# Layer 0 of a hybrid decoder trunk in a new order: phase tables made while x loads, norms first, projections in turn with recurrence steps, and another order of the mixer's tail

## The reference

```python
h = rms_norm(x, norm1)
z = h @ w_in                       # u_a (512), v_b (1024), u_c (512), gates (3 x 1024)
gates = sigmoid(z[..., o3:] + b_gate)
y_a = s5_mixer(u_a, ...) @ ssm_w_proj
y_b = conv_module(v_b, ...)        # GLU, causal depthwise conv of 31 taps, LayerNorm, silu, @ w_proj
y_c = pool_mixer(u_c, ...)         # causal means over 2, 4, 8, 16, minus u_c, grouped matmul, @ w_proj
x = x + (gates[0]*y_a + gates[1]*y_b + gates[2]*y_c) @ w_out
h = rms_norm(x, norm2)
x = x + (silu(h @ w_gate) * (h @ w_up)) @ w_down
```

## Time and profile before

| | us |
|---|---|
| median of 3 runs | 2200.13 (2188.8 to 2464.33) |
| profiled execution | 2193.92 |
| its span (core 5, the slowest; cores 2175.1 to 2192.4) | 2192.4 |
| TensorE busy | 2013.1 |
| VectorE busy | 1013.1 |
| ScalarE busy | 663.8 |

### The profile page before, as it was taken

The page is one execution under the profiler, slowest core; times in us unless marked ns, Lnnn a source line. Parts: engine busy times, 40 slices in busy tenths (PEclk is TensorE's granted clock), DMA queues, the critical chain, the costliest instruction groups (busy, mean ns, idle before and its releaser), DMA issues.

```text
span 2192.4 us, 31111 instructions; the slowest of 8 cores (2175.1 to 2192.4 us)
## 1 busy us (share of the span) xinstructions
PE 2013.1 (92%) x11536; PEld 926.8 (42%) x11536; DVE 1013.1 (46%) x1484; ACT 663.8 (30%) x1104; POOL 85.6 (4%) x160
## 2 busy tenths in 40 slices
PE   2767879999999999999997977999999999999997
PEld 1333344444444444444443434444444444444443
DVE  5647746444454444442252773644445423223226
ACT  3651255222234202314242225622223310110123
POOL 1000000000000000000000000000000000000000
PEclk9978999999999999999998989999999999999998
DMA  9342515222143214224256361522214321322203
GB/s 229 58 103 71 104 28 106 39 39 39 20 135 68 49 29 77 49 54 100 39 190 141 97 121 30 107 39 39 37 22 135 58 39 20 58 39 39 39 10 154
DMA packets 56659, 156.31 MB, mean 71 GB/s; under 512 B 5952, under 2 KB 26816, under 8 KB 53440
## 3 DMA queue, kind: packets, MB, share of 16 engines
q0 software_dynamic: 21456, 77.05, 21.0%
q1 hardware_dynamic: 30448, 73.07, 10.2%
q10 hardware_dynamic: 4608, 4.20, 0.8%
HBM read 191.48 MB, written 27.26 MB: 100 GB/s over the span
## 4 chain that ended last, share of the span: by engine, by line
PE 86%; DVE 5%; ACT 3%; issue 3%; DMA 1%; ACTq 1%; SPq 0%; DVEq 0%
PE ps L257 86%; DVE gt L227 1%; DVE h L235 1%; DMA tab_mid<-ph 1%; ACTq L273 1%; DVE tmp L227 1%; ACT po L246 1%; DMA ud<-stg 0%; ACT sq_s L246 0%; SPq L273 0%; ACT g L246 0%; ACT ps L246 0%; ACT ph L246 0%; DVE lt L227 0%; DVE cv L227 0%
## 5 line engine op out<-in xcount | busy, mean ns | idle before, releaser
L257 PE MATMUL ps<-h,slot 128*128 128x512 bf16 x5376 | 1216.0, 383 | 28.3 <-DVE h L235 18.6
L257 PEld LDWEIGHTS ps<-h,slot 128*128 128x128 bf16 x5376 | 528.0, 99 | 673.0 <-issue 56.5
L227 DVE TENSOR_TENSOR actb<-ps,sgf 128x512 bf16<-128x512 f32 x176 | 121.6, 692 | 418.6 <-PE ps L257 381.5
L257 PE MATMUL ps<-actb,slot 128*128 128x512 bf16 x1408 | 305.9, 379 | 0.0
L246 ACT ACTIVATE sgf<-ps 128x512 f32<-128x512 f32 x176 | 104.8, 595 | 579.6 <-PE ps L257 567.2
L246 ACT ACTIVATE gt<-ps,hb 128x512 f32<-128x512 f32 x192 | 131.4, 686 | 344.8 <-PE ps L257 343.2
L235 DVE SCALAR_TENSOR_TENSOR acc<-gt,ps 128x512 f32<-128x512 f32 x180 | 123.4, 688 | 238.9 <-PE ps L257 235.9
L257 PEld LDWEIGHTS ps<-actb,slot 128*128 128x128 bf16 x1408 | 137.7, 98 | 165.9
L227 DVE TENSOR_TENSOR x<-ps,x 128x512 f32<-128x512 f32 x192 | 130.3, 690 | 133.3 <-PE ps L257 133.2
L264 POOL DMA_DIRECT2D slot<-wts x146 | 77.6, 535 | 1950.3 <-PE ps L257 1911.9
L257 PE MATMUL ps<-mg,slot 128*128 128x512 bf16 x512 | 119.8, 398 | 5.6 <-DVE mg L235 5.6
(11 more groups left out here) (126 smaller groups left out, 1202.7 us busy)
## 6 DMA issues: line engine op xcount, KB each, us to landing
slot<-wts POOLq DMA_DIRECT2D x146, 512.0 KB, 6.8
x<-xT SPq DMA_DIRECT2D x16, 512.0 KB, 18.2
x<-xT SPq DMA_DIRECT2D x4, 2048.0 KB, 19.2
x_mid<-x SPq DMA_DIRECT2D x4, 2048.0 KB, 8.1
x<-x_mid SPq DMA_DIRECT2D x4, 2048.0 KB, 19.2
outT<-x SPq DMA_DIRECT2D x4, 2048.0 KB, 6.3
tab_mid<-ph SPq DMA_DIRECT2D x24, 256.0 KB, 3.4
tab<-tab_mid SPq DMA_DIRECT2D x6, 1024.0 KB, 4.9
```

Of the source, the lines that this page charges most:

```text
L227: return (eng or dve).put(lambda e: e.tensor_tensor(out=out, in0=a, in1=b, op=op), after)
L257: ins = e.matmul(out, lhsT=a, rhs=b, start=start and i == 0, stop=stop and i == n - 1, **kw)
```

## The change

1. **Phase tables.** `rot` becomes part of the beginning of `gens(0)`. The first four phase pairs get a buffer each (in the place of `uc`, not used yet) and are made while x loads, between the small passes for `pk`; SP copies them to `tab`. The last four are made in `tab` itself, by `step(S["rots"])` inside `scan(1)` and `scan(2)`. Layer 0 writes nothing to `tab_mid`.
2. **Norms first.** Squares and `finish` of blocks 0 and 1 come before u; the rest of `gens(0)` moves behind. The `ud` scatter of layer 0 is issued by SP and not by ScalarE, and `k_mid` by ScalarE and not by SP.
3. **u, p, c in turn.** The recurrence of layer 0 starts in the second half of p. In layer 1 all of p comes before c, with 2 steps per part of p from the fifth on and 3 per half-block of c. `out_mats` come before all of `inside`.
4. **Banks.** `bank` takes the bank used longest ago, and `quad` the quad whose last use is oldest (before: a counter).
5. **Tail.** All pool sums stand before conv(0); `cv` has four places of its own (and GT, ACC change theirs); conv(2) goes before glu(0), conv(3) between glu(1) and glu(2), and ln_silu(0) and (1) behind the fold. In the weight order `glu` goes from behind cd 4 to behind cd 6.

The core of the diff (its repeated renamings are left out):

```diff
@@ slot_order
-    if l == 0:
-        order = u + p + c
-    else:
-        order = u + [c[0], p[0], c[1], c[2], p[1], c[3]]
-    order += cd[:5] + [("glu", 0)] + cd[5:] + [("wpc", 0), ("wpc", 1)]
+    order = u + p + c + cd[:7] + [("glu", 0)] + cd[7:] + [("wpc", 0), ("wpc", 1)]
@@ places
-    CV = at("cv", [2, 4, 512], F32, o_rb)
+    CV = [at("cv%d" % i, [4, 512], F32, o) for i, o in enumerate((o_rb, o_rb + 8192, o_x, o_x + 8192))]
-    ACC = [at("acc%d" % i, [3, 512], F32, o_rb + 8192 * i) for i in range(2)]
-    GT = [at("gt%d" % i, [512], F32, o_x + 2048 * i) for i in range(8)]
+    ACC = [at("acc%d" % i, [3, 512], F32, o_x + 8192 * i) for i in range(2)]
+    GT = [at("gt%d" % i, [512], F32, o_rb + 2048 * i) for i in range(8)]
@@ banks
+    def bank():
+        i = min(turn["from"], key=lambda i: turn["at"][i])
+        turn["gen"] += 1
+        turn["at"][i] = turn["gen"]
+        return i
+    def quad():
+        k = min((k for k in (0, 4) if k in turn["from"]), key=lambda k: max(turn["at"][k:k + 4]))
+        turn["gen"] += 1
+        turn["at"][k:k + 4] = [turn["gen"]] * 4
+        return [k, k + 1, k + 2, k + 3]
@@ gens: rot moved to the front, and
+                if l == 0:
+                    t_ld.append([ta, tb])
+                    yield
+                    continue
+        ra = out["ra"] = iter(()) if l else rot(0, 4)
@@ scan
+            drain(S["rots"])
+            want_tabs()
+            rots = iter(())
+            if l == 0 and pt in (1, 2):
+                for i in range(2):
+                    out["ph_free"][2 * pt + 2 + i] = [S["tab_free"][1 - pt % 2]]
+                rots = out["rot"](2 * pt + 2, 2 * pt + 4)
@@ layer 0
-            for b in range(NB):
-                for _ in p_blk(b):
-                    step(g0, 2)
-            turn["from"] = [4, 5, 6, 7]
...
-            for b in range(NB):
-                for i, _ in enumerate(c_blk(b)):
-                    step(g0, 3)
-                    step(sc, 4)
-                    if i == 1 and b:
-                        pool_sums(b - 1)
...
+            for k, _ in enumerate(all_of(p_blk)):
+                step(g0, 1)
+                if k == 7:
+                    turn["from"] = [4, 5, 6, 7]
+                if k >= 7:
+                    step(sc, 2)
+            while "re" not in out:
+                step(g0)
+                step(sc, 2)
...
+            for k, _ in enumerate(all_of(c_blk)):
+                step(g0, 2)
+                want_tabs()
+                step(sc, 4)
+                if k == 5:
+                    pool_edge()
@@ layer 1
-            for _ in range(8):
-                step(cs)
-                step(sc, 3)
-                for _ in range(2):
-                    step(pb)
-                    step(sc, 1)
-            for _ in cs:
-                step(sc, 3)
+            for k, _ in enumerate(all_of(p_blk)):
+                if k > 3:
+                    step(sc, 2)
+                    want_tabs()
+            for _ in all_of(c_blk):
+                step(sc, 3)
+                want_tabs()
@@ tail
+        for m in range(4):
+            pool_sums(m)
         conv(0)
         ln_sum(0)
         conv(1)
         ln_sum(1)
         st2(0)
         ln_stat(0)
         st2(1)
-        st2(2)
         ln_stat(1)
-        st2(3)
         ln_rs(0)
         ln_rs(1)
         ln_apply(0)
         ln_apply(1)
+        st2(2)
+        st2(3)
+        conv(2)
         glu(0)
+        ln_sum(2)
         glu(1)
-        ln_silu(0)
-        ln_silu(1)
-        conv(2)
-        glu(2)
-        ln_sum(2)
-        glu(3)
-        conv(3)
-        ln_stat(2)
-        ln_sum(3)
+        conv(3)
+        glu(2)
+        ln_sum(3)
+        glu(3)
         fold([slot(l, "wpc", h) for h in range(2)])
+        ln_stat(2)
+        ln_stat(3)
+        ln_silu(0)
+        ln_silu(1)
```

More of the change, by code:

```diff
@@ L210, in build_program @@
     W1ST = at("w1st", [4, 2, 2, 128], BF16, o_rb + 4096)
-    KSTS = [[at("kst%d" % i, [4, 2, 128], BF16, o_x + 40960 + 2048 * i) for i in range(4)],
+    KSTS = [[at("kst%d" % i, [4, 2, 128], BF16, o_x + 40960 + 2048 * (i % 3)) for i in range(4)],
             [at("kst", [4, 2, 128], BF16, o_rb + 8192)] * 4]
@@ L615, in gens @@
         out["re"] = [free[0], free[1], free[2], out["kpe"], wc[3][-1]]
-        if l == 0:
-            yield from rot(4, 8)
-        else:
-            ph_free = {n: out["re"] for n in range(3)}
-            out["tab"] = t_ld
+        if l:
+            ph_free.update({n: out["re"] for n in range(3)})
             yield from rot(0, 8)
-        out["end"] = t_ld[5] + t_ld[6] + t_ld[7] + out["w1"] + out["k"]
+        out["end"] = (t_ld[5] + t_ld[6] + t_ld[7] if l else []) + out["w1"] + out["k"]
     def step(g, n=1):
@@ L841, in load_tab, with want_tabs @@
         def load_tab(pt):
+            if l == 0 and pt > 1:
+                S["tab"][pt] = out["tab"][2 * pt] + out["tab"][2 * pt + 1]
+                return
+            if l == 0:
+                pairs = [(TAB[pt][:, k, 2 * i:2 * i + 2], PHS[0][2 * pt + i][:, 1 - k]) for i in range(2) for k in range(2)]
+                S["tab"][pt] = [dmas(sp, pairs, d_tabl[pt], out["tab"][2 * pt] + out["tab"][2 * pt + 1] + S["x1_free"])]
+                S["rd_free"] = S["rd_free"] + S["tab"][pt]
+                return
             S["tab"][pt] = [dma(sp, TAB[pt % 2][:, :], s_tab[l, pt], d_tabl[pt % 2],
                                 [S["tab_free"][pt % 2]] + out["tab"][2 * pt] + out["tab"][2 * pt + 1] + S["x1_free"])]
+        def want_tabs():
+            for pt in range(4):
+                if S["tab"][pt] is None and len(out["tab"]) >= 2 * pt + 2 and pt < S["scanned"] + 2:
+                    load_tab(pt)
         def st2(pt):
@@ L1037, in x_places, with all_of @@
                 S["pt"] = dma(pool, PT[:, :], d_pt[:, :], d_pt_sem, S["x3_free"])
-        def begin_ssm():
-            load_tab(0)
-            load_tab(1)
+        def all_of(blk):
+            for b in range(NB):
+                yield from blk(b)
         def ssm():
@@ L1062, in finish @@
                 x_places()
-            step(g0, 10)
+            step(g0, 6)
+            ra = out["ra"]
+            step(ra, 1)
             squares(0)
+            step(ra, 2)
             finish(0)
-            step(g0, 2)
-            squares(1)
-            S["ws_u"] = [slot(l, "u", c) for c in range(2)]
-            ub = u_blk(0)
+            squares(1)
+            step(g0, 1)
+            finish(1)
+            drain(ra)
+            step(g0, 3)
+            S["ws_u"] = [slot(l, "u", c) for c in range(2)]
@@ L1070, in layer @@
+            load_tab(0)
+            load_tab(1)
+            drain(u_blk(0))
+            step(g0, 2)
+            squares(2)
+            ub = u_blk(1)
+            step(ub, 1)
+            finish(2)
+            drain(ub)
+            squares(3)
+            step(g0, 4)
+            ub = u_blk(2)
+            step(ub, 1)
+            finish(3)
+            drain(ub)
+            step(g0, 4)
+            ub = u_blk(3)
             step(ub, 2)
-            finish(1)
             step(g0, 2)
             drain(ub)
-            squares(2)
@@ new lines, in layer @@
+            S["pads"] = [mset(pool, UC[:, :, :, 0:2], 0.0, S["rd_free"])]
+            S["ws_p"] = [slot(l, "p", c) for c in range(2)]
+            S["ws_c"] = [slot(l, "c", m) for m in range(4)]
+            sc = ssm()
+            S["w1"] = [out["w1"]] * 4
+            S["hp_free"] = lambda pt: S["stg_free"][(0, 1, 4, 5)[pt]]
+            for k, _ in enumerate(all_of(p_blk)):
+                step(g0, 1)
+                if k == 7:
+                    turn["from"] = [4, 5, 6, 7]
+                if k >= 7:
+                    step(sc, 2)
@@ L1186, in layer @@
         S["acce_free"] = [None, None]
+        S["gt_free"] = [S["yb"][i // 4][-1] for i in range(8)]
         ws = (slot(l, "mA", 0), slot(l, "mB", 0))
-        ln_stat(3)
+        merge(0, 0, ws, True)
         ln_rs(2)
         ln_rs(3)
-        merge(0, 0, ws, True)
         ln_apply(2)
@@ L1211, in layer @@
         t_last = last
-        x_load(0, [t_last] + S["gt_free"])
+        x_load(0, [t_last] + S["acc_free"])
         x_load(1, [t_last])
```

195 lines of the change are left out of this document (79 added, 116 removed).

## The result

The changed kernel took 2110.97 us (median of 4 runs, 2107.39 to 2366.68). The kernel before, run beside it, has a ratio to it of 0.9616 (after to before), 95% interval 0.9565 to 0.9667: faster. Disturbed runs are left out of every ratio here, which is why a ratio isn't the quotient of two medians. The profiled execution took 2113.91 us, 1.5 more than its span of 2112.4, 80.0 less than the one before.

What follows compares the result with a forecast made beforehand. TensorE was busy 2013.1 of 2192.4 us, so gains come from its 179 us idle and lower-clock stretches; 47 + 12.5 + 21 + 8.5 = 89 us off 2193.9 gives 2105 us, 8-in-10 range 2080 to 2142.

Steps and rivals of the forecast that it cites:

- The rest: Both merges, w_out and FFN: order kept, x_load(0) about 2 us later but covered by w_out; gain nothing.
- the VectorE budget: Layer 0: 112.0 us of VectorE work after 85.9, so 197.9, and 199 with the first st1.
- the first term: Layer 0 up to the first conv matmul: 212.6 against 259.95, 47 us gained, bounds 30 and 55.
- the second and third terms: Layer 0, conv(0) to merge: 12.5 us gained, bounds 6 and 16; layer 1 up to st2(0): 21, bounds 12 and 25.
- the fourth: Layer 1, st2(0) to merge: 13.5 us idle become 5 to 6; 8.5 gained, bounds 3 and 12.
- The front's walk: Layer 0's start: last norm result 5.0 us earlier, p begins at 86.6 instead of about 93.5, 7 us gained.
- The signs: Right if conv near 212, merge near 290, VectorE above nine tenths busy; wrong if stg waits exceed 1.5 us per half-block.
- the forecast's own case: The whole kernel gains as the terms say, 2105 us within 2080 to 2135; chance 0.76.
- c at 1.2 GHz: Rival, c of layer 0: VectorE's ring halves TensorE's clock, 35 us lost, 2140 us; chance 0.10.
- The early recurrence: Rival, layer 0: scans start only when the inside matrices end, 126 not 102; 24 us lost, 2129; chance 0.06.
- the lost lookahead: Rival, c in both layers: each half-block clears ScalarE and VectorE before the next; net 49 us slower, 2243; chance 0.03.
- The alternation of Sin and Tanh: Layer 0's c on ScalarE: charged nothing; by the skill's page eight switches would cost 21 us, up to 11 on the path.

Runs made afterwards that it cites:

- e4: The changed kernel with layer 1's output and inside matrices in the order of before; 2101.85 us, ratio 0.9594.
- e3: The changed kernel with layer 0's last two kst tiles in stg 3's place, so tg waits only for two k_mid transfers; 2107.55 us, ratio 0.9619.
- e2: The changed kernel with no layer 0 recurrence step ahead of the first c half-block; 2128.94 us, ratio 0.9716.
- best3_again: Rerun on another chip: changed kernel with the edits of e3 and e4 and three recurrence steps per layer 0 c half-block, not four; 2092.9 us, ratio 0.9564.
- e1: The changed kernel with the order of before from st2(0) on in both layers; 2122.07 us, ratio 0.9689.
- e9: The changed kernel with the old PSUM bank rule, a counter for single banks and quads in turn; 2131.93 us, ratio 0.9727.

## Why the prediction was right or wrong

The time was forecast at 2105 us with 2080 to 2142; it came to 2111. The sum was 89 us, the span shows 80. Most mechanisms held; two steps failed. The first is "The rest ... keeps its order ... Nothing": the FFN beside which layer 1's matrices are made did not keep its order, and 9.0 us were given back there (8.7 by e4). The second is the VectorE budget in the first term, 6.5 us too much: VectorE's total was taken for the bound of conv(0), and the wait of the first Tanh for `k_mid` (3.5 us by e3) was left out. That the sum missed by only 9 us is in part luck: on the slowest cores the second and third terms came out 3.1 and 3.8 us larger than forecast, the fourth 2.1 smaller, and 2.0 us behind layer 1's merge were in no term, beside 9.3 given back on these cores. (Merge is counted here, as in the prediction, from its first matmul; the table's marker is its third product.)

**Layer 0 to conv(0)**, 47 forecast, 40.5 on the slowest core (41.9 by the median). The front's walk held: the four `h` start at 29.67, 39.04, 60.17 and 72.43 (29.8, 39.3, 59.8, 72.3). The first recurrence step comes at 105.11, not near 102: VectorE waits 2.35 us for `wc`, queued behind evacuations on ScalarE. Two waits of 0.59 and 2.34 us for inside matmuls follow, then 3.58 for the Tanh behind `k_mid`, which the walk doesn't mention; e3 shows it cost 3.5. The c half-blocks at 4.7 us were right (139.64 to 208.65 is 4.6 each for 15), the allowance of 4 us for Tanh behind phase passes was used by those waits instead. The sums took 14.0 us (205.41 to 219.44) against 12.6 in the walk, with 72 matmuls at the lower clock. The false step is that VectorE must have finished all its steps ahead of conv(0): e2 and best3_again show the last steps under the sums and the conv, and so does the prediction's own figure for the kernel before, where the last recurrence ended at 274.9 us and conv(0) started at 259.95. The evacuation that ScalarE held behind the `tab_mid` stall was one of p and not of c (`stg` from ScalarE; c's first `tg` comes at 161.47); the stall and its end are as the prediction says.

**Conv(0) to merge of layer 0**, 12.5 forecast, 15.6 on the slowest core. The waits left were as named (1.68 for gelu's evacuation, about 3 in fold), the slot of `mB` 0 stayed hidden. Where it came from was half seen: 6.7 from the order (e1), 5.6 from the choice of banks (e9), the rest open.

**Layer 1.** Up to st2(0) 24.8 us less from st1(0) on (137.0 to 112.2), 21 forecast; to merge 6.4 less (68.9 to 62.5), 8.5 forecast. The mechanisms held: the five half-blocks of p took 5.2 us of work out of the stretch behind st1(0) (14.58 us of waiting became 4.32 and 6.10), and the sums' cover for hc is worth 10.4. Mis-sized was p's place, 12.2 us with the wait for `tmp` that it saves.

**The rest at nothing.** The 9.0 us given back beside the FFN come from an edit in `gens` that I had followed in layer 0 only.

**The signs.** conv(0) was at 219.4 and not near 212, merge at 293.8 (near 290 said), VectorE busy 87.33 of the 97 us from 102 to 199, just the nine tenths. TensorE waited 16.2 us for `stg` in c and ahead of the second sum, 1.0 per half-block; none of the signs of being wrong appeared. The range of the forecast's own case, 2080 to 2135, isn't the plain sum of the terms' bounds, which is 2086 to 2143.

**Rivals.** c at 1.2 GHz: no, the clock was 0.96 in 160 to 200. The early recurrence did happen, and its price is 6.3 us at conv(0), not 24. Of the lost lookahead there is no trace: the changed kernel waits 16.2 us for `stg`, the one with the old bank rule 19.1, each with its wait at the pool sums counted in. The alternation of Sin and Tanh costs nothing: between the load at 137.43 and the next at 238.37 ScalarE shows none, while `tab` and `tg` passes alternate. The rule of the Trainium skill (ScalarE: Activation LUTs, "Table sets: the hidden batching unit") is to batch by set; the rows show no switch between Sin and Tanh, so the rule has no case here and isn't refuted. The figure of about 2.66 us a switch that the Trainium skill gives there ("What ACT_TABLE_LOAD costs") isn't what the rows show: a load takes 1.28 us, and the next function starts 1.29 or 1.30 us after the load's start (11.59 and 12.88, 39.46 and 40.76 us).

**What was not tried.** The phase tables through `tab_mid` with everything else changed (their places are now used by p's staging), so the share of that stall in the 42 us is argued, not shown. Undone one at a time the late recurrence, the sums, the banks, the weave and the tail move the median span by 8.2, 25.5, 19.0, 13.7 and 12.2, 78.6 in sum, beside a gain of 80 and 7 to 9 given back; this leaves about 10 for the front and the stall, if they add up.

## What to carry to other kernels

Follow an edit in a shared generator at every place where it is driven: an order that suits one stage starves another through an in-order queue. Work that an engine owes by some point is a bound only for what that point reads; ask which banks and buffers the next matmul needs, and let the rest run past it. A rule that hands out the bank whose last use is oldest was worth 19 us here, more than the new order of the tail (12). Compare waits only with the same waits counted in, and look at the clock of every core before a stretch is called full.

## What the hardware showed that I had not expected

The same 72 pool matmuls behind the same wait did not cost the same on every core of one execution. In the changed kernel, core 6 (as above, 5.54 us) and core 0:

```profile
210.23 4.09 PE L254 MATMUL ps<-uc,pt 128*32 128x512 bf16 x72 [2.90 <-DVE edge L224]
```

Cores 0 and 1 took 4.09 and 4.08 us, cores 2, 4 and 6 took 5.41 to 5.54. On core 6 the granted clock fell to 0.50 from 210 to 212 us; on cores 0 and 1 it stayed at 1.00 from 200 to 213. How full TensorE was ahead of the wait doesn't tell which: core 0 had been busy 31.55 of 40 us and core 6 32.92, while in best3_again cores 5 and 6 had both been busy 31.14 of 32, and took 4.08 and 5.39 behind waits of 2.90 and 2.74. So a gap of under 3 us may or may not cost 1.3 to 1.5 us more, and what decides it stays open.

The third level of the clock, 0.81, is described with best3_again above.

Four scattering transfers took 9.55 us to issue on ScalarE's queue, where the three groups ahead of them had taken 3.30, 2.68 and 2.78.
